# A two-layer encoder on one core: SBUF places of the matmul operands, with block weights and gated activations 96 bytes off

## The reference

```
for each of 2 layers:
    h = x + 0.5 * swiglu(rmsnorm(x)):  (silu(n @ wg) * (n @ wu)) @ wd,   1024 -> 2816 -> 1024
    p = rmsnorm(h) @ w_in                                    1024 -> 3584
    h = h + concat(retention(p), diff_attention(p)) @ w_out  1024 -> 1024
    h = h + 0.5 * swiglu(rmsnorm(h))
    x = rmsnorm(h)
```

## Time and profile before

| | us |
|---|---|
| median of 3 runs | 1901.95 (1901.64 to 1902.09) |
| profiled execution | 1902.16 |
| its span | 1900.3 |
| TensorE busy in the span | 1882.2 |
| GpSimd busy | 1207.8 |
| VectorE busy | 1137.4 |
| ScalarE busy | 906.3 |

### The profile page before, as it was taken

One profiled execution on the slowest core, in us unless ns is written; L12 is line 12 of the kernel. 1 busy time (PEld: TensorE's weight loads), 2 busy tenths in 40 slices (PEclk: granted clock), 3 DMA queues, 4 the chain that ended last, 5 costly groups with the idle time before them and its releaser, 6 DMA issues.

```text
span 1900.3 us, 29706 instructions
## 1 busy us (share of the span) xinstructions
PE 1882.2 (99%) x11550; PEld 1677.2 (88%) x11550; DVE 1137.4 (60%) x1857; ACT 906.3 (48%) x1449; POOL 1207.8 (64%) x814
## 2 busy tenths in 40 slices
PE   9999999999999999999999999999999999999997
PEld 7989989888888989989889898998788889899896
DVE  7727657448745745727676476663586377366273
ACT  7525445456425534524565254444564265255252
POOL 6867767555435867857468586765544277678582
PEclk9999999999999999999999999999999999999999
DMA  4433423232223232323224223223222133323231
GB/s 157 137 100 124 133 84 112 78 100 67 67 67 111 89 112 89 105 97 105 84 101 158 74 104 113 88 89 111 78 68 77 45 111 112 111 90 134 68 109 69
DMA packets 54999, 186.46 MB, mean 98 GB/s; under 512 B 6440, under 2 KB 7976, under 8 KB 54860
## 3 DMA queue, kind: packets, MB, share of 16 engines
q1 hardware_dynamic: 53136, 181.61, 28.9%
q10 hardware_dynamic: 1724, 2.96, 0.4%
HBM read 182.44 MB, written 3.15 MB: 98 GB/s over the span
## 4 chain that ended last, share of the span: by engine, by line
PE 88%; POOL 6%; DVE 2%; ACT 2%; issue 1%; DMA 0%; SPq 0%; DVEq 0%; ACTq 0%; POOLq 0%
PE bank L691 17%; PE bank L693 17%; PE bank L692 17%; PE pair L691 9%; PE pair L693 9%; PE pair L692 9%; POOL w_lo L594 1%; PE pair L986 1%; POOL w_lo_x L613 1%; POOL w_lo L613 1%; PE pair L1014 1%; PE bank L971 1%; PE bank L1026 1%; PE bank L729 1%; PE bank L738 1%
## 5 line engine op out<-in xcount | busy, mean ns | idle before, releaser
L585 POOL TENSOR_TENSOR w_lo<-raw,w_hi 128x512 fp32r<-128x512 f32 (+1 forms) x240 | 315.6, 1340 | 384.9 <-ACT w_hi L1093 384.8
L691 PE MATMUL bank<-hg_hi,w_hi 128*128 128x256 f32 (+1 forms) x1396 | 447.0, 320 | 0.7 <-DVE bank L1575 0.7
L692 PE MATMUL bank<-hg_lo,w_hi 128*128 128x256 f32 (+1 forms) x1396 | 441.3, 316 | 0.0
L693 PE MATMUL bank<-hg_hi,w_lo 128*128 128x256 f32 (+1 forms) x1396 | 441.2, 316 | 0.0
L691 PEld LDWEIGHTS bank<-hg_hi,w_hi 128*128 128x128 f32 x1396 | 264.8, 190 | 22.0 <-issue 5.0
L692 PEld LDWEIGHTS bank<-hg_lo,w_hi 128*128 128x128 f32 x1396 | 265.0, 190 | 18.2 <-issue 1.2
L693 PEld LDWEIGHTS bank<-hg_hi,w_lo 128*128 128x128 f32 x1396 | 265.0, 190 | 17.6
L1093 ACT ACTIVATE w_hi<-raw 128x1024 fp32r<-128x1024 f32 (+1 forms) x120 | 124.2, 1035 | 264.3 <-PE bank L693 126.9
L1542 DVE SCALAR_TENSOR_TENSOR h<-pair,h 128x512 f32<-128x512 f32 x100 | 68.9, 690 | 259.4 <-PE pair L693 259.2
L691 PE MATMUL pair<-a_hi,w_hi 128*128 128x512 f32 x440 | 172.7, 393 | 1.9 <-issue 1.1
L693 PE MATMUL pair<-a_hi,w_lo 128*128 128x512 f32 x440 | 171.7, 390 | 0.0
(11 more groups left out here) (291 smaller groups left out, 4895.5 us busy)
## 6 DMA issues: line engine op xcount, KB each, us to landing
raw<-in_w_gu SPq DMA_DIRECT2D x96, 512.0 KB, 3.7
raw_x<-in_w_gu SPq DMA_DIRECT2D x80, 512.0 KB, 3.9
raw<-in_w_p SPq DMA_DIRECT2D x56, 512.0 KB, 3.5
raw_x<-in_w_dn SPq DMA_DIRECT2D x32, 512.0 KB, 3.8
raw<-in_w_dn SPq DMA_DIRECT2D x32, 512.0 KB, 3.6
raw<-in_w_o SPq DMA_DIRECT2D x16, 512.0 KB, 3.4
raw_x<-in_w_dn SPq DMA_DIRECT2D x16, 384.0 KB, 3.4
raw<-in_w_dn SPq DMA_DIRECT2D x16, 384.0 KB, 3.4
```

The source lines that it names most:

```text
L585: ins = pool.tensor_tensor(columns(lo_[:, part, :]), source[:, part.start * P:part.stop * P], columns(hi[:, part, :]).bitcast(F32), ALU.su ...
L691: pe.matmul(out, hi[:, 0, :], m_hi, start=first, stop=False)
L692: pe.matmul(out, hi[:, 0, :], m_lo, start=False, stop=False)
L693: return pe.matmul(out, lo_[:, 0, :], m_hi, start=False, stop=last)
```

## The change

Only places in SBUF change; each instruction, wait and DMA stays as it is, with other addresses.

- An unused buffer of 896 bytes (LEAD) goes before h, and the DMA scratch shrinks from 16,384 to 1,024 bytes. h, hg_hi and hg_lo then begin at 0 modulo 1024.
- An unused buffer of 96 bytes goes before a_hi, and one of 928 bytes behind a_lo: a_hi and a_lo begin at 96 modulo 1024, and raw again at 0.
- Each slot of w_hi, w_lo, w_hi_x and w_lo_x grows by 128 bytes (SLOT_GAP). Slot s of w_hi begins at 128 s modulo 1024, of w_lo at 512 + 128 s.
- An unused buffer of 288 bytes (SMALL_REST) lies before raw_x. Slots 4 and 5 begin at 0 and 128 modulo 1024 in w_hi_x and at 256 and 384 in w_lo_x; mix_hi and mix_lo begin at 512.
- All weights of fast tiles, in whatever slot, are written and read 96 bytes behind the slot's start (`fast_tiles`, FAST_SHIFT of 24 words). The other weights stay at the slot's start.

```diff
+SLOT_GAP = 32
+FAST_SHIFT = 24
+A_SHIFT = 24
...
+LEAD = 224
+SMALL_REST = 72
...
+        sb("lead", [P, LEAD])
         h = sb("h", [P, KD, T])
         hg_hi = sb("hg_hi", [P, KD, T], F32R)
         hg_lo = sb("hg_lo", [P, KD, T], F32R)
+        sb("a_lead", [P, A_SHIFT])
         a_hi = sb("a_hi", [P, UT, T], F32R)
         a_lo = sb("a_lo", [P, UT, T], F32R)
+        sb("a_rest", [P, 256 - A_SHIFT])
         raw = sb("raw", [P, RAW * UT * P])
-        w_hi = sb("w_hi", [P, SLOTS, UT, P], F32R)
-        w_lo = sb("w_lo", [P, SLOTS, UT, P], F32R)
+        w_hi = sb("w_hi", [P, SLOTS, UT * P + SLOT_GAP], F32R)
+        w_lo = sb("w_lo", [P, SLOTS, UT * P + SLOT_GAP], F32R)
...
+        sb("small_rest", [P, SMALL_REST])
...
-            w_hi_x = sb_ffn("w_hi_x", [P, 2, UT, P], F32R)
-            w_lo_x = sb_ffn("w_lo_x", [P, 2, UT, P], F32R)
+            w_hi_x = sb_ffn("w_hi_x", [P, 2, UT * P + SLOT_GAP], F32R)
+            w_lo_x = sb_ffn("w_lo_x", [P, 2, UT * P + SLOT_GAP], F32R)
...
-        def w_tiles(s, n=UT, at_=0):
-
-            hi, lo = (w_hi[:, s], w_lo[:, s]) if s < SLOTS else (w_hi_x[:, s - SLOTS], w_lo_x[:, s - SLOTS])
-            return hi[:, at_:at_ + n, :], lo[:, at_:at_ + n, :]
+        def w_tiles(s, n=UT, at_=0, shift=0):
+
+            words = slice(shift + at_ * P, shift + (at_ + n) * P)
+            if s < SLOTS:
+                hi, lo = w_hi[:, s, words], w_lo[:, s, words]
+            else:
+                hi, lo = w_hi_x[:, s - SLOTS, words], w_lo_x[:, s - SLOTS, words]
+            return hi.rearrange("p (a b) -> p a b", b=P), lo.rearrange("p (a b) -> p a b", b=P)
+
+        def fast_tiles(s, n=UT, at_=0):
+
+            return w_tiles(s, n, at_, FAST_SHIFT)
...
-            def three(out, w, m_hi, m_lo, first, last):
+            def three(out, w, m_hi, m_lo, first, last, tiles=w_tiles):
 
-                hi, lo_ = w_tiles(w[0], 1, w[1])
+                hi, lo_ = tiles(w[0], 1, w[1])
...
-                    last = three(prod[q], (w, KH * half + k), m_hi[:, k, :], m_lo[:, k, :], k == 0, k == KH - 1)
+                    last = three(prod[q], (w, KH * half + k), m_hi[:, k, :], m_lo[:, k, :], k == 0, k == KH - 1,
+                                 fast_tiles)
...
-    nc = bacc.Bacc("TRN2", target_bir_lowering=False, num_devices=1)
+    nc = bacc.Bacc("TRN2", target_bir_lowering=False, num_devices=1, dynamic_dma_scratch_size=1024)
```

More of the change, by code:

```diff
@@ L430, in raw_block, with w_tile @@
             return source[:, at_:at_ + KH * P]
-        def w_tiles(s, n=UT, at_=0):
-            hi, lo = (w_hi[:, s], w_lo[:, s]) if s < SLOTS else (w_hi_x[:, s - SLOTS], w_lo_x[:, s - SLOTS])
-            return hi[:, at_:at_ + n, :], lo[:, at_:at_ + n, :]
+        def w_tiles(s, n=UT, at_=0, shift=0):
[7 more added lines that the diff above has]
+            return w_tiles(s, n, at_, FAST_SHIFT)
+        def w_tile(part, s, k):
+            return part[:, s, k * P:(k + 1) * P]
         def simple_slot(e):
@@ L592, in lo_gate @@
                 pool.wait_ge(g_hi, at(g_hi, l, m + 1))
-                hi, lo_ = w_tiles(FAST_SLOTS[place(c, i) % 2][0])
+                hi, lo_ = fast_tiles(FAST_SLOTS[place(c, i) % 2][0])
                 pool.tensor_tensor(columns(lo_), raw_tiles(RAW_AT["t", m, 0], UT), columns(hi).bitcast(F32),
@@ L610, in lo_differences @@
                 pool.wait_ge(t13_hi, at(t13_hi, l, m + 1))
-                hi, lo_ = w_tiles(FAST_SLOTS[place(c, i) % 2][1])
+                hi, lo_ = fast_tiles(FAST_SLOTS[place(c, i) % 2][1])
                 both = (raw_x if place(c, i) % 2 == 0 else raw)[:, :].rearrange("p (a b) -> p a b", a=2)[:, :, 0:KH * P]
@@ L619, in lo_b22 @@
                 pool.wait_ge(b22_hi, at(b22_hi, l, m + 1))
-                hi, lo_ = w_tiles(FAST_SLOTS[place(c, i) % 2][2], KH, KH)
+                hi, lo_ = fast_tiles(FAST_SLOTS[place(c, i) % 2][2], KH, KH)
                 pool.tensor_tensor(columns(lo_), raw_block(c, i, 1, 1), columns(hi).bitcast(F32),
@@ L708, in fresh_product @@
                 for k in range(UT):
-                    pe.matmul(out, w_hi[:, s, k, :], m_hi[:, k, :], start=k == 0, stop=False)
-                    pe.matmul(out, w_hi[:, s, k, :], m_lo[:, k, :], start=False, stop=False)
+                    pe.matmul(out, w_tile(w_hi, s, k), m_hi[:, k, :], start=k == 0, stop=False)
+                    pe.matmul(out, w_tile(w_hi, s, k), m_lo[:, k, :], start=False, stop=False)
                 pe.wait_ge(lo_done, at(lo_done, l, u + 1))
                 for k in range(UT):
-                    last = pe.matmul(out, w_lo[:, s, k, :], m_hi[:, k, :], start=False, stop=k == UT - 1)
+                    last = pe.matmul(out, w_tile(w_lo, s, k), m_hi[:, k, :], start=False, stop=k == UT - 1)
                 return last
@@ L728, in first_two @@
                             tile_hi(k)
-                        pe.matmul(outs[s], w_hi[:, s, k, :], hg_hi[:, k, :], start=k == 0, stop=False)
+                        pe.matmul(outs[s], w_tile(w_hi, s, k), hg_hi[:, k, :], start=k == 0, stop=False)
                 for s in range(2):
@@ L732, in first_two @@
                     for k in range(EARLY):
-                        pe.matmul(outs[s], w_lo[:, s, k, :], hg_hi[:, k, :], start=False, stop=False)
+                        pe.matmul(outs[s], w_tile(w_lo, s, k), hg_hi[:, k, :], start=False, stop=False)
                 for s in range(2):
@@ L737, in first_two @@
                             tile(k)
-                        pe.matmul(outs[s], w_hi[:, s, k, :], hg_lo[:, k, :], start=False, stop=False)
+                        pe.matmul(outs[s], w_tile(w_hi, s, k), hg_lo[:, k, :], start=False, stop=False)
                 for s in range(2):
@@ L759, in moving_low @@
                         pe.wait_ge(hg_ready, at(hg_ready, 0, k + 1))
-                    pe.matmul(outs[s], w_hi[:, s, k, :], hg_lo[:, k, :], start=False, stop=False)
+                    pe.matmul(outs[s], w_tile(w_hi, s, k), hg_lo[:, k, :], start=False, stop=False)
                 def weight_low(s, k, last=False):
-                    return pe.matmul(outs[s], w_lo[:, s, k, :], hg_hi[:, k, :], start=False, stop=last)
+                    return pe.matmul(outs[s], w_tile(w_lo, s, k), hg_hi[:, k, :], start=False, stop=last)
                 pe.wait_ge(hi_done, at(hi_done, 0, 1))
@@ L785, in first_units @@
                 pe.wait_ge(hg_ready, at(hg_ready, 0, KD))
-                pe.matmul(outs[0], w_hi[:, 0, KD - 1, :], hg_lo[:, KD - 1, :], start=False, stop=True).then_inc(gu_done, 1)
+                pe.matmul(outs[0], w_tile(w_hi, 0, KD - 1), hg_lo[:, KD - 1, :], start=False, stop=True).then_inc(gu_done, 1)
                 moving_low(1, KD - 1)
@@ L1109, in hi_gate @@
                 slot_free(l, f, c, i, 0, 2)
-                act.activation(columns(w_tiles(FAST_SLOTS[place(c, i) % 2][0])[0]), raw_tiles(RAW_AT["t", m, 0], UT),
+                act.activation(columns(fast_tiles(FAST_SLOTS[place(c, i) % 2][0])[0]), raw_tiles(RAW_AT["t", m, 0], UT),
                                ACT.Copy).then_inc(g_hi, 1)
@@ L1117, in hi_differences @@
                 both = (raw_x if place(c, i) % 2 == 0 else raw)[:, :].rearrange("p (a b) -> p a b", a=2)[:, :, 0:KH * P]
-                hi = columns(w_tiles(FAST_SLOTS[place(c, i) % 2][1])[0]).rearrange("p (a b) -> p a b", a=2)
+                hi = columns(fast_tiles(FAST_SLOTS[place(c, i) % 2][1])[0]).rearrange("p (a b) -> p a b", a=2)
                 act.activation(hi, both, ACT.Copy).then_inc(t13_hi, 1)
@@ L1124, in hi_b22 @@
                 slot_free(l, f, c, i, 2, 3)
-                hi, _ = w_tiles(FAST_SLOTS[place(c, i) % 2][2], KH, KH)
+                hi, _ = fast_tiles(FAST_SLOTS[place(c, i) % 2][2], KH, KH)
                 act.activation(columns(hi), raw_block(c, i, 1, 1), ACT.Copy).then_inc(b22_hi, 1)
@@ L1142, in hi_t2 @@
                 slot_free(l, f, c, i, 2, 4)
-                act.activation(columns(w_tiles(FAST_SLOTS[place(c, i) % 2][2], KH)[0]), t_sum, ACT.Copy).then_inc(x_hi, 1)
+                act.activation(columns(fast_tiles(FAST_SLOTS[place(c, i) % 2][2], KH)[0]), t_sum, ACT.Copy).then_inc(x_hi, 1)
             def hi_t4(l, f, c, i):
@@ L1605, in lo_t @@
                 dve.wait_ge(x_hi, at(x_hi, l, 2 * m + which + 1))
-                hi, lo_ = w_tiles(FAST_SLOTS[place(c, i) % 2][2], KH)
+                hi, lo_ = fast_tiles(FAST_SLOTS[place(c, i) % 2][2], KH)
                 dve.tensor_tensor(columns(lo_), t_sum, columns(hi).bitcast(F32), ALU.subtract).then_inc(x_lo, 1)
```

## The result

| | before | after |
|---|---|---|
| median, us | 1902.02 (6 runs) | 1909.87 (6 runs) |
| ratio, 95% interval | | 1.0043 (1.0032 to 1.0054) |
| span of the profiled execution that the rows come from, us | 1900.3 | 1908.4 |

The kernel became 7.9 us slower. The forecast was 1890 and faster. In one of the six executions of after, the profiled one, TensorE was granted a mean clock of 0.68 and the kernel took 2560 us (the median of the other five is 1909.83), so the rows of after come from a second profile of the same kernel, at 0.999 (1910.31 us, median of 4).

What follows compares the result with a forecast made beforehand. TensorE, busy 99% of the span, was taken as the bound. From 1902.2 us, 7.1 for fast products after waits and 4.6 for down and output projections were subtracted, giving 1890.5, forecast as 1890 us; range 1874 to 1912.

Steps and rivals of the forecast that it cites:

- Fast products: All 6720 matmuls of 256 columns come to distance 32, priced at 280.0 ns: 11.8 us gained before waits.
- no difference between slots: Sign of a right forecast: hg with w and mix with w_x fall to about 280 ns, alike in all slots.
- What becomes late: TensorE catches up with GpSimd's 10.53 us tile cycle and waits before p6; 7.1 of the 11.8 us remain.
- Down and output projections: 512-column matmuls with a: w rows stay at 389 ns at distance 96, only w_x gains, 4.6 us.
- The rival with the bad phase: Down projections at 512 columns lock at 395 ns at distance 96: 9.9 us lost, 1905.0 us; chance 0.20.
- Leads, gaps, smaller scratch: Layout padding is free: projections and first two tiles' 512-column matmuls stay at distance 0 modulo 128; cost 0.
- The rival of the longer period: Conflict repeats over 256 bytes or more, so every second slot falls on a new distance: 31.7 us lost, 1927 us; chance 0.14.
- The rule of the ports: Two independent SBUF read ports make addresses free, so the time stays 1902 us; under the nothing-moves rival, chance 0.10.
- it is the distance that counts: Matmul cost follows weights-to-moving-operand distance, not absolute place: distance 0 gives 282.5 and 282.0 ns at offsets 0 and 96.

Runs made afterwards that it cites:

- The kernel with the shorter cycle: Against the kernel with 256-byte gaps and only fast weights shifted (distance 32), GpSimd skips half of one block's low parts per fast tile: 1878.76 us, 0.9874.
- the fastest complete one: Against the changed kernel: slot gaps 256 bytes instead of 128, fast weights 224 bytes behind their slots (distance 32), gated activations unshifted: 1887.79 us, 0.9924.
- the sweep: Against the changed kernel: 256-byte gaps, gated activations unshifted, each of six slots with its own shift for fast and other weights; two kernels, 1905.42 and 1914.48 us.

## Why the prediction was wrong, by its steps

**Fast products: right in direction, the price somewhat high.** The term was 11.8 us; at equal counts 9.9 was measured (1.5 ns for each matmul, not 1.8). That it came so near is in part luck: the sum put all of them at one distance, with "no difference between slots", and they came to two, 160 modulo 256 in even slots (118.1 ns) and 32 in odd ones (116.8), both below the mean of before (118.9).

**What becomes late: right in mechanism and size.** 4.7 us were to be taken back (11.8 - 7.1), and 4.2 were. GpSimd's cycle stayed at 10.54 us, and p6 of the last tile of chunk 1 had to wait, 0.3 us where the sum had 0.43. The kernel with the shorter cycle shows that this is the limit and not only the order of events. Of the 7.1 us net, 5.7 came.

**Down and output projections: the step that failed.** "I take the value of distance 0, 389 ns": it is 395. The term was -4.6 us, and +10.2 was measured, 14.8 of the 19.4 us between forecast and result. Of these, 8.0 come from the shift of a and 2.2 from the gaps (588.1, 580.1 and 577.9 us with both, with the gaps alone, and before); the other 4.6 are the forecast gain. The rival with the bad phase had +9.9 for it. I chose by the row at distance 96, which had 256 columns, though my own rows showed that at distance 32 the sign turns with the width; and modulo 256 that row stood at 224, not at 96. The width decides: at 512 columns multiples of 256 bytes were the best places tried (16 came near), at 256 columns they were, with 96 and 144, the worst. In the trace of before all 512-column rows off distance 0, of a and of hg, stood at 394 to 398 ns; that was the nearer evidence.

**Leads, gaps, smaller scratch, "cost taken: 0": failed too.** It was +4.1 us for hg at 512 columns, whose distances are 0 in even slots and 128 in odd ones. The sentence that all of these stay at distance 0 was not right even modulo 128: 96 of the 1728 take their weights from slot 5 and stood at 32. I reduced modulo 128, which the trace of before could not justify, since its distances were 0, 32 and 224 modulo 256; the statement in the rivals that 96 stood there "plus multiples of 256" is wrong. The rival of the longer period named this, but priced it at 31.7 us with the fast products among the losers; at 256 columns odd slots gain too. With no shift at all, the layout alone costs 7.0 us (1909.0 against 1902.0).

**The rule of the ports.** The prediction kept as a rival the Trainium skill's rule that a weight load takes nothing from the running matmul ("TensorE: Matmul & The Clock Gate", section "Step-by-step: what each phase is for"). The runs do not bear out what the rival drew from it, that the addresses are free: the kernels with gaps of 128 and 256 bytes and no shift issue the same instructions, and a with w takes 393 ns in the one and 389 in the other; the spacings of all matmuls with a sum to 580.1 and 572.1 us. That it is the weight load which takes this time from the running matmul is not shown.

Together: 1890.5 + 14.8 + 4.1 + 1.4 (the fast products' 5.7 us where 7.1 was forecast) = 1910.8, where 1910.3 was measured.

What stays open is the mechanism itself. The runs show the cost by distance and width, and that at 512 columns it repeats for distances 256 bytes apart (the slots of the kernel with all distances at multiples of 256 are all at 227 to 228 ns). At 256 columns something else has a share, since distance 32 gave 118.0 ns in one layout and 116.7 in another. Between these two both operands of those matmuls had moved by 128 bytes modulo 256, but so had much else; no run moves both alone, so whether their absolute place counts stays open. The prediction's "it is the distance that counts" rested on two figures at distance 0 alone. Which access meets which, and why 256 columns prefer what 512 dislike, no run shows.

## What to carry to other kernels

When TensorE is full and its matmuls of one shape have different durations in rows that differ only by a buffer, sort these matmuls by the distance from the weights to the moving operand and by width, and apply a finding only to the width that it was seen at. Let a layout experiment move one operand at a time, with slots that all stand alike, since a gap of 128 bytes for an unrelated shift cost as much here as the shift gained. And before spending a gain on the full engine, read the cycle of the next one: here some 40% of it came back as waits on GpSimd's cycle (4.2 of 9.9 us in the changed kernel, 8.6 of 21.9 in the fastest complete one).

## What the hardware showed beyond that

- At 512 columns a float32r matmul starts 227.2 ns after the one before when the distance is a multiple of 256 bytes, 232 to 234 ns at most other distances; at 256 columns it is 120.0 ns at multiples of 256 and 116.7 at 32, in the kernels with gaps of 256 bytes.
- At 256 columns the distance is not the whole cause: 192 had 115.3 ns in one slot of the sweep, 116.9 when all slots had it and 117.5 with GpSimd's cycle shortened; 32 had 118.0 ns in the kernel before and 116.7 later.
- The layout with gaps of 256 bytes, fast weights at distance 32 and all else at 0 runs in 1887.8 us, a ratio of 0.9924 to the kernel before.
